# Expert outputs: from a slot table with a combining stage to gated accumulating scatters into the residual

## What is computed

```python
x = x + y_cat @ w_out[l]
x = x + _hier_moe(_rmsnorm(x, norm_ffn_g[l]), ...)
return _rmsnorm(x, norm_final_g)
# inside _hier_moe: top-1 of 4 groups, then top-2 of 8 experts of it: 32 experts, 4096 assignments
a = jax.nn.silu(xblk @ w1[e]) * (xblk @ w3[e])          # a block is 128 rows of one expert
yb = a @ w2[e]
y = jnp.zeros((n_tok, d)).at[sorted_tok].add(yb[dest] * sorted_gate[:, None])
```

## Time and profile before

| | |
|---|---|
| median of 3 runs | 2384.04 us (2378.58 to 2388.4) |
| the profiled execution | 2386.92 us, its span 2385.2 us |
| mean TensorE clock granted | 0.939 |
| DMA moved | 495.69 MB, mean 208 GB/s |

### The profile page before, as it was taken

The page is one execution under the profiler, slowest core; times in us unless marked ns, Lnnn a source line. Parts: engine busy times, 40 slices in busy tenths (PEclk is TensorE's granted clock), DMA queues, the critical chain, the costliest instruction groups (busy, mean ns, idle before and its releaser), DMA issues. The chain is left out here.

```text
span 2385.2 us, 30462 instructions
## 1 busy us (share of the span) xinstructions
PE 2066.8 (87%) x9037; PEld 1492.7 (63%) x9038; DVE 1254.3 (53%) x1133; ACT 1137.5 (48%) x1340; POOL 254.4 (11%) x243
## 2 busy tenths in 40 slices
PE   3997999999997686969999289999999999999910
PEld 2655777777665221327778168888877888888800
DVE  7553232235666443744444554657688646645546
ACT  6771222226665231433332064657698746756623
POOL 0560000000000120320000000000000000000032
PEclk9997999999999798979999689999999999999955
DMA  5563234431110897856432176778899867777478
GB/s 184 168 215 104 92 121 152 130 100 38 38 38 18 319 360 309 275 194 225 154 124 91 49 296 227 255 290 299 334 355 399 296 235 272 275 261 264 167 282 307
DMA packets 260539, 495.69 MB, mean 208 GB/s; under 512 B 25328, under 2 KB 104148, under 8 KB 256085
## 3 DMA queue, kind: packets, MB, share of 16 engines
q1 hardware_dynamic: 218102, 392.01, 46.1%
q10 hardware_dynamic: 30560, 59.78, 7.0%
q0 software_dynamic: 11808, 43.00, 4.9%
HBM read 363.63 MB, written 131.07 MB: 207 GB/s over the span
## 5 line engine op out<-in xcount | busy, mean ns | idle before, releaser
L1645 PE MATMUL p<-wh_hi,x_hi 128*128 128x512 f32 x768 | 309.3, 403 | 11.2 <-DVE wh_lo L1770 11.1
L1770 DVE TENSOR_TENSOR wh_lo<-w_raw,wh_hi 128x2048 fp32r<-128x2048 f32 x128 | 284.7, 2286 | 51.7 <-ACT wh_hi L1734 50.8
L1645 PE MATMUL p<-wh_hi,x_lo 128*128 128x512 f32 x768 | 304.5, 396 | 0.0
L1645 PE MATMUL p<-wh_lo,x_hi 128*128 128x512 f32 x768 | 304.5, 396 | 0.0
L508 PE MATMUL pj<-h_hi,wp_hi 128*128 128x512 f32 x640 | 257.0, 402 | 12.7 <-DVE wp_lo L685 12.7
L508 PE MATMUL pj<-h_lo,wp_hi 128*128 128x512 f32 x640 | 254.2, 397 | 0.0
L508 PE MATMUL pj<-h_hi,wp_lo 128*128 128x512 f32 x640 | 254.1, 397 | 0.0
L1734 ACT ACTIVATE wh_hi<-w_raw 128x2048 fp32r<-128x2048 f32 x128 | 234.5, 1914 | 0.2
L1645 PEld LDWEIGHTS p<-wh_hi,x_hi 128*128 128x128 f32 x768 | 144.9, 189 | 49.7 <-DVE wh_lo L1770 15.1
L1645 PEld LDWEIGHTS p<-wh_hi,x_lo 128*128 128x128 f32 x768 | 144.8, 189 | 35.1
L1645 PEld LDWEIGHTS p<-wh_lo,x_hi 128*128 128x128 f32 x768 | 145.1, 189 | 32.8
(11 more groups left out here) (285 smaller groups left out, 3575.2 us busy)
## 6 DMA issues: line engine op xcount, KB each, us to landing
w_raw<-in_exp_w_dram SPq DMA_DIRECT2D x512, 256.0 KB, 4.6
w_raw<-in_exp_w_dram SPq DMA_DIRECT2D x128, 512.0 KB, 10.2
scratch_YB<-yb ACTq DMA_DIRECT2D x50, 512.0 KB
scratch_KA<-work SPq DMA_DIRECT2D x32, 512.0 KB, 3.0
scratch_YB<-zero SPq DMA_DIRECT2D x4, 4096.0 KB
kin<-scratch_KA SPq DMA_DIRECT2D x32, 512.0 KB, 7.3
arena<-scratch_SA SPq DMA_DIRECT2D x32, 512.0 KB, 6.0
scratch_SI<-arena SPq DMA_DIRECT2D x32, 512.0 KB, 3.7
```

The source lines that it names most:

```text
L1645: mm = pe.matmul(acc[:, :], x[:, k, :], w, start=(k == 0 and i == 0), stop=(k == n - 1 and i == 2))
L1770: dve.tensor_tensor(lo, raw[:, j:j + 2, :], hi.bitcast(F32), ALU.subtract).then_inc(lowered, 1)
```

## The change

The table `YB` goes, with its zero fill, and with it the gathers and the adding in the last stage. Instead `route` also makes, for each slot, its gate (`weight`) and the row of the residual it belongs to (`spot`; a slot that is not used points at one of 128 extra rows of `X2`, a different one on each partition). In `experts` ACT copies with `weight` as scale, and POOL scatters `yb` to the rows of `X2`, adding to what is there. The last stage `final_norm` loads all 16 tiles into SBUF of their own, without a buffer to wait for, and normalises in place.

```diff
@@ project_and_lru: the fill and its wait go
-                if j % 3 == 0 and j // 3 < CT:
-                    fill(j // 3)
...
-            sp.wait_ge(filled, 16 * CT)
...
@@ route
+            for c in range(2):
+                pe.wait_ge(row_ready, BASE + c + 1)
+                pe.wait_ge(col_ready, BASE + c + 1)
+                for t in range(NT):
+                    last = pe.matmul(pw[:, 0:IDX_COLS], row[:, c, t, :], col[:, c, t, :],
+                                     start=(c == 0 and t == 0), stop=(c == 1 and t == NT - 1))
+            last.then_inc(weight_mm, 1)
...
+            for c in range(2):
+                act.wait_ge(hit, BASE + 2 * c + 2)
+                act.activation(row[:, c, :, :], row16[:, c, :, :], ACT.Copy).then_inc(row_ready, 1)
...
+                dve.tensor_tensor(col[:, c, :, :], hit16[:, :, :], over_last(gates[:, c, :], IDX_COLS), ALU.mult).then_inc(col_ready, 1)
+                dve.wait_ge(col_ready, BASE + c + 1)
             dve.wait_ge(idx_mm, BASE + 1)
-            step(dve.tensor_copy(idx[:, :], pr[:, 0:IDX_COLS]))
+            step(dve.tensor_scalar(idx[:, :], pr[:, 0:IDX_COLS], 1.0, 1.0, ALU.max, ALU.subtract))
+            step(dve.tensor_scalar(blank[:, :], pr[:, 0:IDX_COLS], 0.0, pad[:, 0:1], ALU.is_equal, ALU.mult))
+            step(dve.scalar_tensor_tensor(out=spot[:, :], in0=pr[:, 0:IDX_COLS], scalar=-1.0, in1=blank[:, :], op0=ALU.add, op1=ALU.add))
+            dve.wait_ge(weight_mm, BASE + 1)
+            step(dve.tensor_copy(weight[:, :], pw[:, 0:IDX_COLS]))
...
@@ experts: POOL
+            def scatter(B):
+                pool.wait_ge(y_evac, BASE + B + 1)
+                pool.tensor_copy(cur_spot[:, :], spot[:, ds(B, 1)]).then_inc(spot_ready, 1)
+                pool.wait_ge(spot_ready, BASE + B + 1)
+                pool.sem_inc(pool_passed, 1)
+                pool.indirect_dma_start(out=rows, out_offset=bass.IndirectOffsetOnAxis(ap=cur_spot[:, :], axis=0),
+                                        in_=yb[:, :], in_offset=None, compute_op=ALU.add).then_inc(y_out, 16)
+
+            def added(B):
+                pool.wait_ge(y_out, B * 16 + 16)
+                pool.sem_inc(y_added, 1)
...
             def body(e, B):
+                scatter(B)
                 gather_after(B + 1)
+                added(B)
 
             B = per_block(pool, "pool", body)
+            for last in range(2):
+                scatter(B + last)
+                added(B + last)
...
@@ experts: ACT
                 act.wait_ge(y_done, BASE + B + 1)
-                act.wait_ge(y_out, BASE + B * 16)
+                act.wait_ge(y_added, BASE + B)
                 for c in range(2):
-                    copy = act.activation(yb[:, c * 512:(c + 1) * 512], py[c][:, :], ACT.Copy)
+                    copy = act.activation(yb[:, c * 512:(c + 1) * 512], py[c][:, :], ACT.Copy, scale=weight[:, ds(B, 1)])
                 copy.then_inc(y_evac, 1)
-                act.wait_ge(y_evac, BASE + B + 1)
-                act.dma_start(dram["YB"][ds(B * P, P), :], yb[:, :]).then_inc(y_out, 16)
...
```

More of the change, by code:

```diff
@@ L1405, in _, with route @@
                 add_bias(t)
-def route(nc, dram, LG, gates, slots, idx, nblk, ident):
+def route(nc, dram, LG, weight, idx, spot, nblk):
     NL = N_GROUPS + N_EXP
@@ L1805, in _ @@
         def _(sp):
-            sp.dma_start(gain[:, :], dram["norm_final_g"].partition_broadcast(P)).then_inc(gain_in, 16)
-            def load(t, q):
-                sp.dma_start(x[:, q, :], dram["X2"][ds(t, 1)].rearrange("a p d -> (a p) d")).then_inc(x_in[q], 16)
-            for q in range(4):
-                load(q, q)
-            def store(t, q):
-                sp.wait_ge(o_ready, BASE + t + 1)
-                for g in range(2):
-                    sp.dma_start(out_t[ds(t, 1), g].rearrange("a n d -> (a n) d"), out[HALF * g:HALF * g + HALF, q % 2, :]).then_inc(o_out[q % 2], 16)
@@ L1817, in _ @@
-            with sp.Fori(0, NT // 4 - 1) as it:
-                for q in range(4):
-                    store(it * 4 + q, q)
-                    load(it * 4 + q + 4, q)
-            for q in range(4):
-                store(NT - 4 + q, q)
-            for s in range(2):
-                sp.wait_ge(o_out[s], BASE + 32 * (NT // 2))
-        @block.gpsimd
-        def _(pool):
-            for t in range(NT):
-                if t >= 4:
-                    pool.wait_ge(s2, BASE + t - 3)
-                for c in range(2):
-                    pool.indirect_dma_start(out=y[:, t % 4, c, :], out_offset=None, in_=dram["YB"],
-                                            in_offset=bass.IndirectOffsetOnAxis(ap=slots[:, c, t:t + 1], axis=0)).then_inc(y_in[t % 4], 16)
+            for t in range(NT):
+                sp.dma_start(x[:, t, :], dram["X2"][t]).then_inc(x_in[t], 16)
+                if t == 0:
+                    sp.dma_start(gain[:, :], dram["norm_final_g"].partition_broadcast(P)).then_inc(gain_in, 16)
@@ L1875, in step, with invert @@
-            def step(t, q, ahead=True):
-                if ahead:
-                    add_expert(t + 1, (q + 1) % 4, 0)
-                root(t, q)
-                if ahead:
-                    add_expert(t + 1, (q + 1) % 4, 1)
-                scale(t, q)
-            for c in range(2):
-                add_expert(0, 0, c)
-            with dve.Fori(0, NT // 4 - 1) as it:
-                for q in range(4):
-                    step(it * 4 + q, q)
-            for q in range(4):
-                step(NT - 4 + q, q, ahead=q < 3)
+            def invert(t):
+                dve.wait_ge(squared, t + 1)
+                dve.tensor_scalar(st[:, t, 1:2], st[:, t, 0:1], 1.0 / D, EPS, ALU.mult, ALU.add).then_inc(mean, 1)
+                dve.wait_ge(mean, t + 1)
+                dve.reciprocal(st[:, t, 2:3], st[:, t, 1:2]).then_inc(inverse, 1)
@@ L1893, in routing_tables @@
+            invert(0)
+            for t in range(NT):
+                if t + 1 < NT:
+                    invert(t + 1)
+                dve.wait_ge(root, t + 1)
+                if t == 0:
+                    dve.wait_ge(gain_in, 16)
+                dve.scalar_tensor_tensor(out=x[:, t, :], in0=x[:, t, :], scalar=st[:, t, 3:4], in1=gain[:, :],
+                                         op0=ALU.mult, op1=ALU.mult).then_inc(o_ready, 1)
 def routing_tables():
@@ L1924, in build @@
             output_projection(nc, dram, LG, w_hi, w_lo, ident)
-        route(nc, dram, LG, gates, slots, idx, nblk, ident)
-        experts(nc, dram, nblk, idx, ident)
-        combine(nc, dram, gates, slots)
+        route(nc, dram, LG, weight, idx, spot, nblk)
+        experts(nc, dram, nblk, idx, spot, weight, ident)
+        final_norm(nc, dram)
 _INS = ["x", "norm_mix_g", "w_in", "lru_conv_w", "lru_conv_b", "lru_wr_f", "lru_br_f", "lru_wi_f", "lru_bi_f", "lru_lambda_f",
```

83 lines of the change are left out of this document (25 added, 58 removed).

## The result

The changed kernel takes **2352.26 us** (median of 4 runs, 2351.17 to 2354.09) against 2386.22 of the kernel before (4 runs, 2378.58 to 2390.53): a ratio of 0.9866, 95% interval 0.9852 to 0.9879, 34 us faster. The forecast was 2354. The profiled execution took 2352.69 us, its span is 2350.9, at a mean granted clock of 0.946.

The account below looks back on a forecast made before the run. PE was taken to set the pace of `experts`, with DMA level in 16 blocks, and DMA to bound the last stage. 9.3 + 6.5 + 5 − 52.5 = −31.7 gave 2352 against the median 2384.0, rounded up to 2354; range 2338 to 2390.

Parts of the forecast that it names:

- `route`: Stage ahead of `experts`, all on the path: constant 0.5, DVE product 1.3, float32 matmuls 7.5; +9.3 us (9 to 16).
- by columns 68 of 128 gives 0.113 us: Float32 matmuls in `route`: step time scales with columns, so 64 x 0.117 = 7.5 us; 13.6 if weight loading sets the pace.
- `experts`, ACT and POOL: Blocks of `experts`: ACT's slightly longer copies are hidden, and POOL's scatter issue doesn't delay the gather; 0 us.
- latency covered up to some 16 us: Blocks of `experts`: next `store_y` comes 12 us after the scatter's issue, ACT has 4.6 more; a gather lands in 7.3.
- `experts`, DMA: Blocks where DMA is level with PE: the scatter's extra read lengthens runs of such blocks; +6.5 us (0 to +70).
- x: Extra DMA time per block in `experts` for the accumulating scatter's read of old rows: 1.3 us (0 to 6).
- the lead: Level blocks of `experts`: loads are 3.9 us early per run; x eats this first, then each block grows by x.
- The end of `experts`: From the last copy to the next stage's first issue: POOL 1.5, longer landing 2.7, copies and semaphores; +5 us (2 to 9).
- The last stage: `final_norm` moves 17.3 MB instead of 34.1: 45 us of bytes plus 5, 50 instead of 102.5; −52.5 us (−55 to −45).
- the adding doesn't hold the engines: Rival for the level blocks: adding holds the DMA engines, change slower once a scatter takes over 5.4 us; 19%.
- DMA is not level: Rival for `experts`: the stretches take more bytes without a block growing, and the last stage runs at 400 GB/s; 2343; 14%.
- All of 0.21 us is paid: Rival: `route`'s float32 steps cost 0.21 us each and the last stage reaches only 334 GB/s; 6 + 7 us more, 2367; 8%.

Follow-up runs that it names:

- experiment 4: The changed kernel with the four zero fills of 4 MB put back into the projection, into a table nobody reads: 2351.31 us (one run).
- experiment 3: The changed kernel with 34 instead of 68 columns in the float32 matmuls of `route`: 2350.65 us (one run).
- experiment 5: The changed kernel with the gates sent through PE as two f16 parts instead of float32: 2343.49 us (4 runs), ratio to the kernel before 0.9829.
- experiment 1: The changed kernel with a scatter that overwrites the residual's rows instead of adding to them: 2352.42 us (one run).
- Experiment 2: The changed kernel with a second accumulating scatter per block, of the same rows, to 128 spare rows: 2391.76 us (one run).
- experiment 10: The changed kernel with the very last block's rows stored by ACT's plain DMA instead of scattered, their adding left out: 2340.89 us (one run).
- experiment 9: The kernel before, with POOL also waiting at the end of `experts` for ACT's last store to land: 2389.82 us (one run).
- experiment 7: The changed kernel with the last stage's old buffers (four to load, two to store) and old store order: 2380.27 us (10 runs), ratio to before 0.998.

## Why the prediction was right, term by term

The time came out 2 us from the forecast, and that close only by luck, since errors of +6.4 (`route`), −7.7 (`experts`), +6.3 (its end) and −5.1 us (last stage) cancel. What was right is which stages pay and that the last one gains far more; against the sum of −31.7 the −34.3 lack only the 2.5 us that lie ahead of `route`.

*The zero fill,* 0 us: experiment 4 shows nothing else, within the spread of the traces.

*`route`,* +9.3 predicted, +15.7 measured. The step that failed is "by columns 68 of 128 gives 0.113 us". The upper bound, named beside it, was the truth: 64 steps of 0.217 us. The trace had shown both numbers, 0.21 us at 128 float32 columns and 0.056 at 68 f16 columns, and I drew the line through the columns; in experiment 3 half the columns took the same time, with PEld busy throughout. The reason given for 7.5, that loading was hidden in f16, doesn't carry over: experiment 5 has f16 weights at 0.060, and float32 weights load in 0.215.

*`experts`, ACT and POOL,* 0 us: right in the sum. But the "latency covered up to some 16 us" was too generous. A scatter takes 9.1 us in a level block where I had the gather's 7.3, and in 16 blocks ACT was ready for its next copy 6 to 8 us after the scatter's issue, not the 12 of the block that I had read. So ACT's copies waited for the landing 16 times, 33 us in all. PE waited for such a copy once, for 2.4 us; the rest is hidden behind PE.

*`experts`, DMA,* +6.5 predicted. x itself is right in the level blocks: 1.3 predicted, 1.34 measured between experiment 1 and the change. What was mis-sized is the lead, 3.9 us. The run of six grew by 0.9 by PE's work (1.9 by its window, 1.0 of it given back) instead of 3.9; 6x − lead = 0.9 makes the lead some 7 us. Up to the last matmul the stage is no longer at all (−1.2, inside the 2 us by which its first two blocks differ between executions; from the third gather to the last it is 1.1 us longer, 862.8 instead of 861.7). Experiment 2 is the case of x = 3.9: by the formula 6 x 3.9 − 3.9 = 19.5 us for the run of six, and it took 131.37 − 111.25 = 20.1. A lead of 7 would give 16.4 there, so one lead for both cases leaves 3.7 us. In that run the granted clock was 0.96 and the matmuls took 4.8 us more, and PE waited 10.8 us for ACT's copies; either can be the rest, which wasn't tried apart, so the agreement with 19.5 may be chance. By the prediction's estimate from *Collectives: The Full Stack* of the Trainium skill, Part 3 (a reducing transfer at half the rate of a copy), a scatter takes 2.5 us; by that rule, the trace agrees in the level blocks, within one core as well (2.6 against 1.3). For the last scatter, alone on the engines, it does not (3.5 against 1.3), and there the measurement decides.

*The end of `experts`,* +5 predicted (2 to 9), +9.5 from the copy's end measured, just beyond the bound. POOL between copy and issue is +1.3 of it (1.5 were predicted). For the other 8.2 us the prediction had a longer landing, 2.7, and 0.8 for slower copies and more semaphores. What the runs showed is that they hang on a scatter by POOL as the last act (experiment 10, where the same semaphores cost nothing), and that POOL as the last to wait costs 4.1, which no row of before showed, with no scatter at all (experiment 9). A landing of 6.2 us against 2.6 for a plain store, +3.6, would leave only 0.5 over; but in experiment 1 the last transfer was done 3 us sooner and the gap stayed, so that this part is not shown and the split stays open. Another 1.6 us, the last copy's wait for the scatter ahead, wasn't thought of.

*The last stage,* −52.5 predicted, −57.6 measured. The bytes and the landings were reckoned as 45 + 5 us; together they took 45.0, since DMA ran at 410 to 430 GB/s in nearly all of the stage, where I had taken 400 from the level blocks, and what lies around it was short. The words "no load waits for a buffer" were worth more than the prediction says: with the old buffers it was 72 us, and the whole change, at 2380, won 4 us (experiment 7). An argument by bytes alone would have been wrong.

The rivals: the adding doesn't hold the engines (2.6 us, not over 5.4). "DMA is not level" is refuted by experiment 2, though at x = 1.3 the result looks like it. "All of 0.21 us is paid" came true in its first half; the last stage's rate did not.

## What to carry to other kernels

Less traffic shortens a DMA stage only as far as its buffers let the queue run full: work out the buffers' cycle (here a store's landing per output buffer) beside the bytes. For tiny products with new weights at each step, f16 parts can be far cheaper than one float32 product; read the price per step at the same type, not per column. At a stage's end look at which engine comes last: a scatter by POOL there cost 9.5 us more than a plain store by ACT. Experiment 10 avoided all of it, but left the last block's adding out; a kernel that also does that adding elsewhere was not tried.

## What the runs showed that was not expected

- A float32 matmul step at the half clock took 0.217 us with 68 columns and with 34, of which the load of its weights was 0.215; an f16 step with 68 columns took 0.056 to 0.060.
- An accumulating scatter of 512 KB took 2.6 us of all 16 engines in level blocks and 3.5 alone; a plain one took 1.3 in both places. It was issued in 1.6 us against 0.99, and landed in 6.2 us on an empty queue where a plain store took 2.6.
- POOL as the last engine to wait in a stage delayed the next by 4.1 us (9.8 against 5.7), with no work of its own.
- With POOL's scatters as the last act and POOL waiting, the next stage's first load came 14.9 to 15.5 us after the last copy, whether the transfer took 1.3, 3.5 or 6.2 us of the engines.
